# First expert's rows through a 0/1 slot table, with the job table built beside its up products

## What is computed

```python
x = layer_norm(DEEPNORM_ALPHA * x + mix, ln1_g, ln1_b)
logits = x @ router_w + router_b
top_v, top_i = lax.top_k(logits, TOP_K)            # 4 of 32 experts for each row
gates = jax.nn.softmax(top_v)
for e in range(N_EXPERTS):                         # rows of x that chose e
    hh = xb @ e_w_in[e] + e_b_in[e]                # 1024 -> 2048: "up"
    gate, up = jnp.split(hh, 2)
    act = clip(gate) * sigmoid(1.702 * clip(gate)) * (clip(up) + 1)
    y += gates * (act @ e_w_out[e] + e_b_out[e])   # 1024 -> 1024: "down"
x = layer_norm(DEEPNORM_ALPHA * x + y, ln2_g, ln2_b)
```

## Time and profile before

| | |
|---|---|
| time, median of 3 runs | 1348.16 us (1344.98 to 1349.28) |
| the profiled execution | 1353.49 us, its span 1351.7 us |
| PE busy | 1183.2 us (88%) |
| DVE busy | 515.8 us (38%) |
| moved by DMA | 463.19 MB, mean 343 GB/s |

### The profile page before, as it was taken

One profiled execution on the slowest core, in us unless ns is written; L12 is line 12 of the kernel. 1 busy time (PEld: TensorE's weight loads), 2 busy tenths in 40 slices (PEclk: granted clock), 3 DMA queues, 4 the chain that ended last, 5 costly groups with the idle time before them and its releaser, 6 DMA issues.

```text
span 1351.7 us, 34179 instructions
## 1 busy us (share of the span) xinstructions
PE 1183.2 (88%) x12540; PEld 523.4 (39%) x12541; DVE 515.8 (38%) x875; ACT 272.8 (20%) x533; POOL 244.5 (18%) x214
## 2 busy tenths in 40 slices
PE   7998999937899999998899989989898989999760
PEld 6886545512233333432233423332333332533210
DVE  2996637764232222232223232420423320432226
ACT  0003233410102230141121211130121211131213
POOL 4000001331111221142120311221121212120113
PEclk9998899958999999999999999999999999999765
DMA  9702831549999999999999999999999999999963
GB/s 358 199 3 85 295 152 34 231 147 410 415 419 412 409 413 410 417 391 414 417 410 415 410 412 413 383 406 416 416 408 414 410 419 371 390 406 419 412 218 129
DMA packets 79977, 463.19 MB, mean 343 GB/s; under 512 B 12324, under 2 KB 20873, under 8 KB 29709
## 3 DMA queue, kind: packets, MB, share of 16 engines
q1 hardware_dynamic: 69083, 438.76, 80.2%
q0 software_dynamic: 8768, 17.47, 5.1%
q10 hardware_dynamic: 2066, 6.32, 1.2%
HBM read 447.51 MB, written 19.48 MB: 345 GB/s over the span
## 4 chain that ended last, share of the span: by engine, by line
PE 51%; DMA 22%; issue 3%; DVE 2%; ACT 0%; SPq 0%; DVEq 0%; ACTq 0%; POOLq 0%; POOL 0%
PE pu L1865 32%; PE rest L1879 17%; DMA ring<-in_e_in 13%; DMA ring<-in_e_out 8%; PE pu L1859 1%; PE rest L1890 1%; DVE fin L2081 0%; DVE bn L2063 0%; DVE xgT L2002 0%; DVE mv L2074 0%; DMA fin<-acc_rows 0%; DMA acc_rows<-y,row 0%; PE rest L1884 0%; SPq L281 0%; DMA xq<-x_rows,idx 0%
## 5 line engine op out<-in xcount | busy, mean ns | idle before, releaser
L1865 PE MATMUL pu<-ring,xgT 128*32 128x512 f32 x5248 | 587.9, 601 | 35.9 <-DMA ring<-in_e_in 35.2
L1865 PEld LDWEIGHTS pu<-ring,xgT 128*32 128x32 f32 x5248 | 161.8, 111 | 444.1 <-issue 443.3
L1879 PE MATMUL rest<-ring,hid 128*32 128x256 f32 x5248 | 302.2, 388 | 23.8 <-DMA ring<-in_e_out 16.3
L2032 DVE TENSOR_SCALAR gg<-pu 128x1280 f32<-128x1280 f32 x32 | 47.7, 1492 | 604.6 <-PE pu L1865 604.6
L1789 POOL DMA_INDIRECT acc_rows<-y,row x82 | 110.7, 1350 | 747.7 <-ACT y L1945 731.5
L1879 PEld LDWEIGHTS rest<-ring,hid 128*32 128x32 f32 x5248 | 168.7, 112 | 147.6 <-issue 46.1
L1945 ACT ACTIVATE y<-rest,gate 32x256 f32 x328 | 152.8, 466 | 297.1 <-issue 293.4
L1925 ACT ACTIVATE ss<-gg 128x1280 f32<-128x1280 f32 x32 | 40.7, 1272 | 537.7 <-DVE gg L2032 537.7
L866 PE MATMUL pair<-xt,ring 128*128 128x260 f32 x448 | 101.2, 388 | 7.3 <-DMA ring<-in_w_in 5.6
L1779 POOL DMA_INDIRECT xq<-x_rows,idx x82 | 88.2, 1075 | 91.9 <-issue 80.0
L866 PEld LDWEIGHTS pair<-xt,ring 128*128 128x128 f32 x448 | 86.2, 193 | 21.2 <-DMA xt<-in_xT 7.4
(11 more groups left out here) (270 smaller groups left out, 547.7 us busy)
## 6 DMA issues: line engine op xcount, KB each, us to landing
ring<-in_e_in SPq DMA_DIRECT2D x256, 1024.0 KB, 24.2
ring<-in_e_out SPq DMA_DIRECT2D x128, 1024.0 KB, 25.5
ring<-in_w_in SPq DMA_DIRECT2D x3, 1536.0 KB, 24.7
ring<-in_w_in SPq DMA_DIRECT2D x5, 512.0 KB, 11.0
ring<-in_w_o SPq DMA_DIRECT2D x1, 2048.0 KB, 12.0
conv<-in_x_prompt SPq DMA_DIRECT2D x1, 2048.0 KB, 13.8
x_rows<-conv ACTq DMA_DIRECT2D x4, 512.0 KB
acc_rows<-conv ACTq DMA_DIRECT2D x4, 512.0 KB
```

Source lines behind the costliest of these rows:

```text
L1865: mm = nc.tensor.matmul(pu[quarter(c), j], xgT[:, j, k], w[:, :, c * QC:(c + 1) * QC], start=False, stop=k == KT - 1, skip_group_check=True)
L1879: mm = nc.tensor.matmul(py[quarter(c), j], hid[:, j, 2 * q + f], w[:, f, c * QC:(c + 1) * QC], start=False, stop=q == FT // 2 - 1 and f == ...
L2032: V.tensor_scalar(gg[:, :, :], pu[:, :, 0], SW_LIMIT, None, ALU.min).then_inc(g_ready, 1)
```

## The change

**Rows of job 0 without a list.** For each tile DVE writes which slot of expert 0 each row has, as a table of 0 and 1 of 160 columns (`first_slots`, two instructions for a tile). PE multiplies these tables with the parts of the row numbers, which gives the row number of each slot: once for tiles 4, 3, 2, 1 together, ahead of `logits(0)`, and once for tile 0, behind the counts. DVE adds the two, makes gather indices of them and the number of groups (`first_size`), and POOL gathers job 0's rows in the first block. It waits for the indices and for the five writes to `x_rows`; the writes to `acc_rows` have a semaphore of their own (`sums_begun`), for which SP waits before the barrier.

**What goes to the second block.** The writing of tile 0's list (four indirect DMAs, now POOL's first work there), the loading of the lists (ACT, all four copies, when all are written), units 7 and 8 of the first expert (SP's first work there), and `job_table` and `job_rows`. DVE turns job 0's rows first and then builds the table; PE runs job 0's up in code of its own ahead of the loop, and the turn of the table's columns (four products) between its unit 3 and its unit 4. All engines then wait for `jobs_ready` before they go on to the loop; DVE waits for the lists after it and names jobs 0, 1 and 2.

**What goes away.** The zeroing of both halves of `xq`, and the zeroing of PSUM in the second block: DVE zeroes all eight banks at the very start of the first block instead, and PE's first use of each bank waits for that (`psum_zero`). Buffers are laid over others to make room (`xq`, `xgT` and `hid` over q, k and v; the table over the last norm's buffer).

The pieces of the diff stand in the order of the code; from the loading of units (7, 8) on they are of the second block: SP, POOL, PE, ACT, DVE.

```diff
-            stepped(sp, "rest1")
-            for j in (7, 8):
-                load_unit(sp, 0, j)
             sp.wait_ge(stored, 16 * (NT + 1 + 4))
             sp.wait_ge(copied, 48)
+            sp.wait_ge(sums_begun, 16 * (NT + 1))
...
-            for i in (NT,) + TILES:
+            for i in (NT,) + TILES[:-1]:
                 list_rows(i, NTH[i])
+            gp.wait_ge(x1_sent, 16 * (NT + 1))
+            gp.wait_ge(first_named, 1)
+            size = gp.value_load(first_size[0:1, 0:1], min_val=1, max_val=JG)
+            x1_quarters = x1_dram.rearrange("r (c n) -> (r c) n", n=QC)
+
+            def gather_first(j):
+                nc.gpsimd.indirect_dma_start(
+                    out=xq[:, 0, j], out_offset=None, in_=x1_quarters,
+                    in_offset=bass.IndirectOffsetOnAxis(ap=idx4[:, 0, j:j + 1], axis=0),
+                    bounds_check=NQ * R - 1, oob_is_err=False).then_inc(gathered, 16)
+                if j + 1 < JG:
+                    with gp.If(size > j + 1):
+                        gather_first(j + 1)
+            gather_first(0)
...
+                a.dma_start(acc_dram[i * P:i * P + rows(i)], src).then_inc(sums_begun, 16)
...
-            a.wait_ge(listed, 16 * TOPK * (NT + 1))
-            for c in (1, 3):
-                a.dma_start(lists[c * GS:(c + 1) * GS, 0:NE * JG], lists_dram[:, 0:NE * JG]).then_inc(lists_in, 16)
-            a.wait_ge(x1_sent, 32 * (NT + 1))
...
+                        pe.wait_ge(psum_zero, 3)
...
+            def first_ids_of(tiles, dst):
+                pe.wait_ge(slots_ready, NTH[tiles[-1]])
+                for j in range(JG):
+                    for i in tiles:
+                        m = rows(i)
+                        for c in range(NQ):
+                            mm = nc.tensor.matmul(dst[c * GS:(c + 1) * GS, j], in_slot[0:m, i, j * GS:(j + 1) * GS],
+                                                  id_parts[0:m, i], start=i == tiles[0], stop=i == tiles[-1],
+                                                  skip_group_check=True)
+                mm.then_inc(ids_done, 1)
...
             turn_rows1(0)
+            pe.wait_ge(s_max, 2 * NSTEPS)
+            first_ids_of((NT,) + TILES[:-1], ids_early)
             logits(0)
             rank(0)
...
+            pe.wait_ge(ids_kept, 1)
+            first_ids_of((0,), ids_last)
...
+            for b in pair:
+                V.memset(b[:, :, :], 0.0).then_inc(psum_zero, 1)
+            for b in bS + bT:
+                ch.mark(V.memset(b[:, :], 0.0))
+            ch.wait()
+            d.engine_nop().then_inc(psum_zero, 1)
...
+            def first_slots(i, ranks):
+                m = rows(i)
+                if i == NT:
+                    d.wait_ge(k_stored[0], 48)
+                    d.wait_ge(k_stored[1], 32)
+                ch.do(V.scalar_tensor_tensor(keys[0:m, i:i + 1], ranks[:, 0:1], 1.0, memb[0:m, i, 0:1], ALU.add, ALU.mult))
+                V.tensor_scalar(in_slot[0:m, i], C("slot", m), keys[0:m, i:i + 1], None, ALU.is_equal
+                                ).then_inc(slots_ready, 1)
...
+                if i:
+                    first_slots(i, ranks)
...
+            d.wait_ge(ids_done, 1)
+            V.tensor_copy(early_ids[:, :, :], ids_early).then_inc(ids_kept, 1)
             root1(0)
             shifted1(0)
             route(0)
             scaled1(0)
+            d.wait_ge(rank_done, NTH[0] - 1)
+            d.wait_ge(m_ready, NTH[0])
+            first_slots(0, ranks_of(0))
...
+            d.wait_ge(counted, 1)
+            ch.do(V.tensor_copy(after0[:, 0:1], totals[0:1, 0:1]))
+            ch.do(V.tensor_scalar(more0[:, 0:JG - 1], C("step", 1)[:, 0:JG - 1], after0[:, 0:1], None, ALU.is_lt))
+            ch.do(V.tensor_reduce(more0[:, JG - 1:JG], more0[:, 0:JG - 1], AX.X, ALU.add))
+            ch.mark(V.tensor_scalar(first_size[:, :], more0[:, JG - 1:JG], 1.0, None, ALU.add))
+            d.wait_ge(ids_kept, 1)
+            d.wait_ge(ids_done, 2)
+            ch.do(V.tensor_tensor(first_ids[:, :, :], ids_last, early_ids[:, :, :], ALU.add))
+            ch.do(V.scalar_tensor_tensor(first_ids[:, :, 0], first_ids[:, :, 1], 4.0, first_ids[:, :, 0], ALU.mult, ALU.add))
+            V.tensor_scalar(idx4[:, 0], first_ids[:, :, 0], float(NQ), C("quarterpad"), ALU.mult, ALU.add
+                            ).then_inc(first_named, 1)
+
+            key, mine, better = beats2, own[:, 0:1], own[:, 1:2]
+            ch.mark(V.scalar_tensor_tensor(key, totals, float(NE), C("tie", NE), ALU.mult, ALU.add))
+            ch.mark(V.tensor_copy(own[:, 2:3], total_column))
+            ch.do(V.scalar_tensor_tensor(mine, total_column, float(NE), C("tie1", NE), ALU.mult, ALU.add))
+            ch.do(V.tensor_scalar(beats, key, mine, None, ALU.is_gt))
+            ch.do(V.tensor_reduce(better, beats, AX.X, ALU.add))
+            ch.mark(V.tensor_scalar(placed[:, 0], C("place", NE), better, own[:, 2:3], ALU.is_equal, ALU.mult))
+            V.tensor_scalar(placed[:, 1], C("place", NE), better, C("job", NE), ALU.is_equal, ALU.mult
+                            ).then_inc(placed_ready, 1)
             weigh(0, NTH[0])
             place(0)
...
+            d.wait_ge(ordered, 1)
+            ch.do(V.tensor_scalar(after0[:, 1:2], after0[:, 0:1], float(JR), None, ALU.is_le))
+            ch.do(V.tensor_scalar(next_expert[:, :], in_order[0:1, NE + 1:NE + 2], after0[:, 1:2], None, ALU.mult))
...
+            for j in (7, 8):
+                load_unit(sp, 0, j)
+            first = sp.value_load(next_expert[0:1, 0:1], min_val=0, max_val=NE - 1)
             for k in range(KT):
                 sp.wait_ge(up_done, k + 1)
                 load_unit(sp, first, k)
...
+            sp.wait_ge(jobs_ready, 1)
...
+            for k in range(TOPK):
+                nc.gpsimd.indirect_dma_start(
+                    out=lists_dram.rearrange("s q c -> (s q) c"),
+                    out_offset=bass.IndirectOffsetOnAxis(ap=spots[:, 0, k:k + 1], axis=0),
+                    in_=pairs[:, 0, k], in_offset=None,
+                    bounds_check=GS * NE * MAXQ - 1, oob_is_err=False).then_inc(listed, 16)
             gp.sem_inc(y_free, 3)
-            for u in range(4):
+            gp.wait_ge(jobs_ready, 1)
+            for u in range(1, 4):
...
+                    if between and k == KT // 2 - 1:
+                        between()
...
+            def turn_fields():
+                pe.wait_ge(fields_ready, 1)
+                for k in range(3):
+                    nc.tensor.matmul(turned_fields[:, k * P:(k + 1) * P], fields[:, k:k + 1], C("ident"),
+                                     start=True, stop=True)
+                nc.tensor.matmul(turned_fields[:, 3 * P:4 * P], fields[:, 0:1], C("tri"), start=True, stop=True
+                                 ).then_inc(fields_turned, 1)
+
+            size = pe.value_load(first_size[0:1, 0:1], min_val=1, max_val=JG)
+            pe.wait_ge(turned, 1)
+            pe.wait_ge(chosen_ready, 1)
+            pe.wait_ge(pu_read, 1)
+            up(size, 1, turn_fields)
+            pe.wait_ge(jobs_ready, 1)
             last = job_count(pe)
...
-            nc.scalar.activation(xq[:, 0].rearrange("p j n -> p (j n)").rearrange("p (a n) -> p a n", n=P),
-                                 C("ones").unsqueeze(1).broadcast_to([P, JG * QC // P, P]), ACT.Copy, scale=0.0
-                                 ).then_inc(xq_zero, 1)
+            a.wait_ge(listed, 16 * TOPK * (NT + 1))
+            for c in range(NQ):
+                a.dma_start(lists[c * GS:(c + 1) * GS], lists_dram).then_inc(lists_in, 16)
             a.sem_inc(y_done, 2)
             sigmoid(0)
+            a.wait_ge(jobs_ready, 1)
...
+            turn_rows(0, d.value_load(first_size[0:1, 0:1], min_val=1, max_val=JG))
+            choose(0)
...
+            job_table()
+            job_rows()
+            d.wait_ge(jobs_ready, 1)
             d.wait_ge(lists_in, 16 * NQ)
             name_rows(ch, 0, 0)
...
-            choose(0)
-            ch.mark(V.memset(pu[:, :, :, :], 0.0))
-            ch.mark(V.memset(py, 0.0))
-            d.wait_ge(more_lists_in, 16 * NQ)
             for u in (1, 2):
                 name_rows(ch, u, d.value_load(jobs[0:1, 2, u:u + 1], min_val=0, max_val=NE * MAXN - 1))
-            turn_rows(0, through(slice(1, 2)))
```

More of the change, by code:

```diff
@@ L272, in C @@
             return cst[0:rows, lo:hi]
+        pu = outer.enter_context(nc.psum_tensor("pu", [P, JG, 2, QC], F32))
+        rest = outer.enter_context(nc.psum_tensor("rest", [P, 3, 512], F32))
         unit_in = [sem(f"unit_in{u}") for u in range(UNITS)]
         lists_in = sem("lists_in")
-        more_lists_in = sem("more_lists_in")
+        placed_in_lists = sem("placed_in_lists")
+        listed = sem("listed")
+        gathered = sem("gathered")
         def load_unit(eng, e, j):
@@ L410, in first_block @@
         taps = chn("taps").rearrange("p (i k) -> p i k", i=3)
```

(35 more changed lines are left out.)

241 lines of the change are left out of this document (113 added, 128 removed).

## The result

| | before | after |
|---|---|---|
| median of 10 runs each, us | 1349.52 (1344.98 to 1351.55) | 1353.08 (1349.47 to 1356.09) |
| ratio after / before | | 1.0029, 95% interval 1.0017 to 1.0041 |
| the profiled execution, us | 1353.49 (first trace), 1345.95 (second trace, run b_again) | 1352.35 |

The forecast was 1341.5 us and faster; the time is 11.6 us above it and outside the range. It is 3.6 us above the kernel before: 0.29%, at the edge of the 0.3% that the prediction counts as no change, with an interval that lies wholly above 1.

A forecast was written before the change was run, and what follows sets the result against it. The prediction took the experts' weight stream, at a fixed DMA rate, as the bound. PE starting 8.3 us earlier, less 1.6 for lists in the stream, gave 6.7 us: median 1348.16 to 1341.5, range 1339.9 to 1343.5 (chance 0.50).

The forecast's parts named there:

- the first part's reading: Experts' stretch, 304 to 1315 us: weights stream at 404 GB/s, and PE's lateness is made up at its next wait.
- In the stream that is free: Job 1's rows, 2 us late, cost the stream nothing: some 3 of 7.3 us of slack are used.
- the sum stays: One code stop at job 1 uses 3.5 of the 4.3 us left, so the gain remains 6.7 us.
- Job 1's rows: After job 0's up begins: lists, naming and POOL's gather under load put these rows 2 us behind DVE's readiness.
- The stops: Loop's copy of up, new to PE at job 1: a wait for code of 3.46 us, as seen once in down.
- The early part: Ahead of tile 0's write to x_rows: added work makes it asked for at 276.1 instead of 274.23, 1.9 us lost.
- The 80 products: Early row numbers on PE, ahead of tile 0's logits: 3.0 us, upper end 6.7.
- The barrier: End of the first block: POOL's drain behind its gather is the last wait, and the barrier goes at 285.1.
- The lists in the stream: Lists, 0.66 MB, asked for at about 294 inside the weight stream instead of in idle DMA time: 1.6 us lost.
- The slower one: Rival, chance 0.09: lists fall behind weights, needing 25 us; an 11 us DMA hole follows near 321; 1352.7 us.
- The two stops at job 1: A second code stop ahead of the first refill at job 1 loses 2.7 us, leaving a gain of 4.0, 1344.2 us.
- the smaller gain: Rival, chance 0.28: early products cost 6.7 us or a 3.46 us stop follows the barrier; gain 3.0 to 3.2, 1345.

The follow-up runs named there:

- b_again: The kernel before, unchanged, run once more for a second trace; it took 1345.95 us.
- a_one_copy: The kernel after with job 0's up back in the loop, at its third place, so PE jumps over code first; 1357.3 us, ratio to before 1.0055.
- a_copy2: The kernel after with one copy of up and job 0 at the loop's first place; 1346.8 us, ratio to before 0.9985.
- a_early: The kernel after with all row-number products behind the counts and POOL reading the number of groups early; 1351.2 us, ratio to before 1.0014.
- a_bytes: The kernel after with 1.57 MB of weights loaded once more into an idle buffer; 1352.2 us, ratio to before 1.0018.
- b_no_bias: The kernel before without the bias products of up; 1348.7 us, ratio to before 0.9996.
- best1: The kernel after with one copy of up, job 0 at the loop's first place, and the early gather; 1343.7 us, ratio to before 0.9970.
- a_split: The kernel after with lists loaded in two parts, each expert's first 160 rows first; 1351.9 us, ratio to before 1.0019.
- a_lists_first: The kernel after with SP waiting for the lists before its first refill; 1349.6 us, ratio to before 1.0003.

## Why the prediction was wrong

**The step that failed** is the first part's reading: "the experts' stretch is a stream of weights at a fixed rate; PE's lateness within it is made up for by the next such wait". It came from a mean over 1011 us, 919 of them busy on PE, and from a misread row: the 25.57 us of the earlier trace rows is a unit's way from asking to landing, not a wait of PE's, which was busy for 29.6 of the 30 us from 760 and for 25.1 of those from 790, and waited there for 1.9 us at most. The stretch has two parts. In the first, from job 2 to about 600 us, PE waits for no weight and has no "next such wait" in which to make up: job 2 began 3.4 to 4.0 us late by tile 3's write, and the median rose by 3.6. From that step followed "In the stream that is free" for job 1's rows and "the sum stays" for the stops. Both things were seen; both were priced at nothing.

**Job 1's rows** were put 2 us late. Measured from PE's first product they were later: the lists took 7.59 us to land beside the first eight refills, and up of job 1 began 26.9 us behind PE's first product (315.09 less 288.22) against 22.5 in the earlier trace rows (319.77 less 297.27) and 21.2 in the second trace: 4 to 6 us late.

**The stops.** The loop's copy stopped at job 1 for 4.35 us where PE had not run it, and did not stop where it had (a_one_copy, a_copy2); first jumps over code took 4.65 to 6.90 us, later ones 0.2. The Trainium skill, *Runtime: NRT & Kernel Launch*, section "Instruction fetch mechanics", says that a taken branch to code outside the window held on chip has to wait for that code to be fetched. These numbers agree with it. The row gave a good size for the stops. What was missed was that they make job 2 late where PE cannot make it up: from up of job 1 to job 2 PE took 31.3 us instead of 24.8 and 26.6.

**The early part**: 1.9 us were forecast to be lost, and tile 0's write came 55.71 us behind tile 3's instead of 53.61 in both traces of before: 2.1. The terms were not those forecast. The 80 products took half of the 3.0 us, but the logits behind them took 3.62 instead of 2.0, at a granted clock of 0.50 (the lower level, 1.2 GHz), and the slot tables of tiles 2 and 1, costed at nothing and at 0.5 us, pushed the writes of these tiles by 0.4 us each:

```profile
265.72 1.49 PE L1043 MATMUL pu<-cpre,ktok 8*32 8x2 bf16 x80
...
267.14 3.62 PE L1093 MATMUL pu<-rw,xt 128*128 128x32 f32 x16
...
267.00:271.00 4.00, 3.76 (x32) 3.61 (x28) 2.66 (x5) 2.21 (x3) 2.88 (x2) 0.50 0.63 246
```

The 80 products are not the whole of that: in a_early, which has none of them ahead of the logits, these took 2.74 us while the granted clock averaged 0.66, against 1.94 to 2.02 us at 0.92 to 1.00 in the two traces of before. Why the clock falls earlier stays open. Of the 2.7 us for tile 0's write, 0.4 cited no row; the gather began 5.0 us behind the ask (274.14 to 279.13) where 4.2 were forecast.

**The barrier** went as forecast, with POOL's drain last (forecast at 285.1, DVE's at about 282):

```profile
L345 DVEq DRAIN  x1: 17/17/17, 279.5 to 279.5; - x1
L345 POOLq DRAIN  x1: 4654/4654/4654, 279.7 to 279.7; - x1
...
L345 POOLq EVENT_SEMAPHORE  x2: 17/17/17, 284.4 to 284.5; - x2
```

PE came at 288.2 where 289.0 was forecast, and the first refill 4.7 us behind it, exactly as read. But that is luck in part, and the comparison with the earlier trace rows flatters it: that trace was 2.2 us later at tile 3's write. By that clock the gain at PE's first product was 6.9 us, where 8.3 was forecast.

**The lists in the stream** were to cost 1.6 us. In the 44 us from the first refill DMA moved 382 GB/s in after against 397 and 400 in before, with a share of 0.99 to 1.00 in all three, and 0.66 MB of that were the lists: (397 x 44 - 382 x 44 + 660) / 404 = 3.3 us (3.6 by the second trace). The bytes were right, not the rate at which they pass; that the whole of the lower rate is the lists' doing is not shown. By the median of a_bytes the end does not feel bytes of this size.

**Right as forecast**: units 7 and 8, asked for at 284.6, were never waited for; the table's columns held PE up nowhere between unit 3 and unit 4; the zeroing at the start was free (PE's first product at 5.61, 5.57 in the earlier trace rows).

**The rivals.** The slower one had the right suspect, the lists, with the wrong mechanism: they took 7.6 us and not 25, and there was no hole at 321. What the end lost was lost at job 2, some 175 us before the hole showed. The two stops at job 1 that were put under the smaller gain did come; the 4.0 us that were to be left of the gain did not, by the step above.

## What to carry to other kernels

Before a wait in a long stretch is called free, cut the stretch into pieces and look in each for the wait that ends last: a mean of 91% on PE hid 250 us at 97% with no wait for data. A transfer's length on the chain is not the wait of the engine behind it. Where two resources are both just in time, an edit must bring both forward: here an earlier stream with a later job 2 (the change) gave nothing, PE's time alone (b_no_bias) gave nothing, and a version that brought forward stream and job 2 (best1) gave 4 to 5 us. Code that is run once ahead of a loop leaves the loop's own code to be fetched later, where that may be on the path; and traces of two kernels are compared from a common event ahead of the edit, not from the span's start.

## What was not expected of the hardware

A first jump over code that PE had not yet run took 6.65 us (over up) and 4.65 us (over down, 6.90 in a_copy2); the same jumps afterwards took 0.2 us. Runs through new code beside a full stream of weights stopped for up to 4.2 us at a time (4.22 us in up of a_split, 4.18 in down of a_lists_first), and queue q8 "instruction" had no packet from job 2's start to 1300 us. And two executions of the same kernel reached tile 3's write at 214.4 and at 220.6 us, which is more than all that the change did to the time.
